# Weight halves split ahead, copies ahead of an exponential, squares kept in attention's order and masks moved, in a two-layer HGRN2 and attention step

## The chip, the cores and the metric

One core of a Trainium2 chip runs the whole kernel in one launch. The metric is the device time in microseconds (us); lower is better. The median of three runs of the kernel before is 1120.97 us (1120.49 to 1121.94).

## What is computed

Two layers are applied to a prompt of 512 rows and to 64 rows of eight sampled sequences, 1024 features each, all in fp32. Both layers have the same frame:

```python
h = rmsnorm(x, norm_w) * (1 + scale) + shift      # shift, scale, gate = silu(c) @ w_ada + b_ada
y = (mixer(h) * silu(z)) @ w_out                  # z: part of the layer's one input projection
x = x + gate * y
```

Layer 0 is a gated linear recurrence with 8 heads (key width 128, value width 256): `S_t = diag(f_t) S_{t-1} + k_t v_t^T`, `o_t = S_t^T q_t`, then an rmsnorm of `o` per head. Layer 1 is windowed attention with 12 heads of 128 in three groups with dilations 1, 4 and 16, with rotated, normalised queries and keys. The outputs are the new rows, the recurrent states, and the key and value rows of layer 1.

## The kernel before

The program is written by hand for five engines: TensorE (PE) multiplies, ScalarE (ACT) copies and evaluates functions, VectorE (DVE) and GpSimd (POOL) do the arithmetic between tiles, and SyncE (SP) issues nearly all transfers. Each engine runs its own list in program order, and semaphores tie the lists together. The order of each list is what the change edits.

**Weights.** They stream from HBM into `raw`, a ring of three slots. ScalarE copies a piece rounded to `w_hi` (`split_hi`, L347) and VectorE writes the rest to `w_lo` (`split_lo`, L355), both in rings of three slots. A product is three matmuls: high by high, high by low, low by high. `split_hi` waits until the piece three before it has been used; for a piece of an output column that is the end of the whole column (`pj_ready`), though the column has two pieces of eight blocks each. Once split, a slot of `raw` is free and SyncE can load the next piece.

**Layer 0, heads.** Step `h` of a loop projects head `h` and scans head `h - 1`. Within it, seven levels of decays are built: VectorE subtracts (`dve_sub`), ScalarE takes the exponential (`level_exps`, L895), VectorE multiplies keys and queries by it (`dve_level`, L867, L868). ScalarE's list also holds the copy of the values out of PSUM (L939) and of the turned keys (L943), both behind exponential 4 (counted from 0) in the steps that also scan. TensorE's chunk states (L1273) need both copies and, except for the last head, the masked keys of VectorE (`masked_keys`, L1098). In step 7, the last that projects, there are no adaLN projections on TensorE's list between the turned keys and the chunk states; steps 1 to 6 have them.

**Layer 0, output.** Eight columns `m` of 128 features, 16 blocks each (L1415). Column 0 is woven into the last scans; column 1's first eight blocks follow before the end of the loop. The second half of column 1 needs the piece `("out0", 1, 1)`. The residual input is parked in HBM and read back (`xT<-xpark`) when the last head is finished (`fin_done`). For each column VectorE adds the residual (`dve_residual`, L1182 to L1186), scales for the next norm (`amplify`, L575) and sums squares; ScalarE squares (`norm_square`, L535), writing in time order.

**Second norm.** TensorE sums squares over the partitions by a matmul with ones (`norm_pe`, L520), reading them through `perm`, which takes the time steps with a stride of 16 elements; its outputs are in the order of attention. ScalarE takes the inverse root (L550, L551), then VectorE scales (L583), ScalarE adds the shift and rounds (L557), VectorE forms the low part (L588), for eight feature blocks, then for the sequences' rows. Behind it VectorE has a weight split, `read_late_ada` (L488, L493), two masks (L2473, L2474) and a memset before its first step in attention.

**Attention.** TensorE starts with `pe_first_rows` as the blocks of `h` appear. `rope_act` sums squares per row, `rope_dve` (L1665, L1672) and `rope_pool` (L1692 to L1697) normalise and rotate; TensorE's next rows in the same PSUM bank (L1707) wait for L1665 and for the next split.

Of the kernel before, what the change touches and what calls it, by code (L numbers as in the profile page):

```python
# [128 lines left out]
def program(nc, I, O):  # L129
    with ExitStack() as ctx:  # L130
# [59 lines left out]
        at_done = sem("at_done")  # L190
# [143 lines left out]
        def split_hi(key):  # L334

            act = nc.scalar
            i = split_no[key][0]
            arrived(act, key)
            if i >= SPLITS:
                old = split_keys[i - SPLITS]  # L340
                if old[0] == "a" and old[2] in (0, 2, 4, 6):
                    act.wait_ge(half_used, 4 * old[1] + old[2] // 2 + 1)
                else:
                    act.wait_ge(pj_ready, split_no[old][1] + 1)
            n = index[key]
            size = stream[n][2] * stream[n][3]
            act.activation(w_hi[:, i % SPLITS, 0:size], raw[:, n % RAWS, 0:size], ACT.Copy).then_inc(hi_done, 1)  # L347
# [163 lines left out]
        def norm_pe(sq, slot):  # L511
            pe = nc.tensor
            if slot == 0:
                pe.wait_ge(sq_sum, 3 + KD - 2)
            else:
                pe.wait_ge(n_sq, 2 * KD)
            turned = perm(sq[:, slot, 0:TP])
            for e in range(2):
                out = X[:, e, 0:TP // 2].rearrange("p (r q i) -> p r q i", r=2, q=4)
                last = pe.matmul(out, ones[:], turned[:, 2 * e:2 * e + 2], start=(slot == 0), stop=(slot == 1))  # L520
                if slot:
                    last.then_inc(n_ms, 1)
            last = pe.matmul(X[:, 2, 0:TS], ones[:], sq[:, slot, TP:T], start=(slot == 0), stop=(slot == 1))
            last.then_inc(n_ms, 1)
# [5 lines left out]
        def norm_square(xT, sq, k):  # L530

            act = nc.scalar
            if k >= 2:
                act.wait_ge(sq_sum, 3 + k - 1)
            act.activation(sq[:, min(k, 1), :], xT[:, k, :], ACT.Square).then_inc(n_sq, 1)  # L535
# [9 lines left out]
        def second_norm_act(act, chain):  # L545
# [19 lines left out]
            split_hi(("a", 0, 2))  # L565
# [13 lines left out]
        def second_norm_dve(dve, chain):  # L579
# [11 lines left out]
            split_lo(("a", 0, 1))  # L591
# [21 lines left out]
            split_lo(("a", 0, 2))  # L613
            read_late_ada(chain)
# [262 lines left out]
        def act_step(act, chain, h):  # L877
# [30 lines left out]
            if end:  # L908
                if h <= AH:
                    logs_and_exps()  # L910
                act.wait_ge(ms_ready, f + 1)
                act.activation(sq0[:, 0, 0:TP], X[:, 0, :], ACT.Ln, bias=eps[:, 0:1], scale=1.0 / ADV)
                act.activation(sq0[:, 0, TP:T], X[:, 1, 0:TS], ACT.Ln, bias=eps[:, 0:1], scale=1.0 / ADV).then_inc(ms_read, 1)
                act.wait_ge(ms_read, f + 1)
                act.activation(sq0[:, 0, :], sq0[:, 0, :], ACT.Exp, scale=-0.5).then_inc(r_done, 1)
            if h == AH:
                oz_hi(6, 12)
                act.wait_ge(gram_ready, 3 * g + 3)
                act.wait_ge(op_ready, g)
                for i in (6, 7):  # L920
                    for s0_, s1_, t0_, t1_ in level_blocks(i):
                        ins = act.activation(at[s0_:s1_, :, t0_:t1_], wide_at(i)[s0_:s1_], ACT.Copy)
                ins.then_inc(at_done, 1)
            if h > AH:
                oz_hi(14, 16)
            if new:
# [10 lines left out]
                level_exps(0, 5 if scan else 6)  # L937
# [3 lines left out]
            if scan:  # L941
                act.wait_ge(kt_ready, g + 1)
                act.activation(kr[:].rearrange("p c k -> p (c k)"), X[:, 3, :], ACT.Copy).then_inc(kr_done, 1)  # L943
                if h == AH:
# [97 lines left out]
        def dve_step(dve, chain, h):  # L1042
# [59 lines left out]
            if new:  # L1102
# [3 lines left out]
                for i in range(8):  # L1106
# [4 lines left out]
                    if i == 5 and scan:  # L1111
                        masked_keys()
# [286 lines left out]
        def pe_out(pe, name, m, blocks):  # L1399
# [3 lines left out]
            for n in blocks:  # L1403
# [9 lines left out]
                for i, (a, b) in enumerate(((wh, o_hi(n)), (wh, lo), (wl, o_hi(n)))):  # L1413
                    for e, (x, z) in enumerate(((0, HP), (HP, T))):
                        last = pe.matmul(PJ[:, 2 * (t % 2) + e, 0:z - x], a[:, n % nk, :], b[:, x:z],  # L1415
                                         start=(n == 0 and i == 0), stop=(n == 2 * nk - 1 and i == 2))
            if blocks and blocks[-1] == 2 * nk - 1:
                last.then_inc(pj_ready, 1)
# [304 lines left out]
        def pe_first_rows(pe):  # L1723
# [40 lines left out]
            pe.wait_ge(ada_done, 4 + AH)  # L1764
# [195 lines left out]
        def pe_attention(pe, j):  # L1960
            a, old = j - 1, j > 0
            for k in range(12 if j < GH - 1 else 8):
                if k == 9:
                    pe.wait_ge(ss_mask, 3 * j + 1)
                if j == 0 and k < 2:
# [267 lines left out]
        def dve_attention(dve, chain, j):  # L2233
# [147 lines left out]
            for k in range(12 if j < GH - 1 else 8):  # L2381
                if k >= 8 or k % 2:
                    split_ahead(split_lo, j, k)
                if old and k == 0:
                    mask_s(a, 1)
                if k < 6:
# [70 lines left out]
        def attention_tables(dve, chain):  # L2457
# [11 lines left out]
            dve.tensor_copy(masks[1][0], masks[1][1])  # L2469

        def attention_masks(dve):

            dve.tensor_copy(masks[0][0], masks[0][1])  # L2473
            dve.tensor_copy(masks[2][0], masks[2][1]).then_inc(tab_done, 1)  # L2474
# [148 lines left out]
        def _(act):  # L2623
# [14 lines left out]
            for m in range(KD):  # L2638
                split_out(split_hi, "out0", m)
                if m == 0:  # L2640
                    split_hi(("out0", 1, 1))
                if m == KD - 1:
                    split_hi(("a", 0, 0))
                    split_hi(("a", 0, 1))
                wait_read(act, OUT0 + m)
                norm_square(xT1, nsq1, m)
# [13 lines left out]
        def _(dve):  # L2660
# [19 lines left out]
            dve.wait_ge(unparked, 16)  # L2680
            dve.tensor_copy(late_scT, scT[:])
            for m in range(KD):
                split_out(split_lo, "out0", m)
                if m == 0:
                    split_lo(("out0", 1, 1))
                if m == KD - 1:
                    split_lo(("a", 0, 0))
                if m == 4:
                    attention_tables(dve, chain)
                dve_residual(dve, chain, 0, OUT0 + m, m, xT1, yg)  # L2690
                amplify(m)
# [3 lines left out]
            attention_masks(dve)  # L2695
# [69 lines left out]
```

## Time and profile before

| | us |
|---|---|
| median of three runs | 1120.97 (1120.49 to 1121.94) |
| the profiled execution | 1122.75 |
| its span, first to last instruction | 1121.1 |
| outside the span | 1.65 |

The profile is one execution, told as a page (busy time of each engine, slices, the chain that ended last, groups of instructions) and as a trace that can be asked for waits, for a stretch in order of time, and for the granted clock of TensorE. Times in it count from the start of the span. A stall is the idle time in front of an instruction, with the event that ended it behind "<-". "issue" is idle time for which the profile shows no releaser. Instructions overlap a little, so the distance from start to start is less than a duration.

### The profile page before, as it was taken

What the parts mean: (1) busy time and instruction counts of PE and PEld (TensorE: products, weight loads), DVE (VectorE), ACT (ScalarE), POOL (GpSimd) and SP (SyncE); (2) the same over time, 40 slices, a digit from 0 to 9 for tenths busy, and PEclk for the clock granted to TensorE, in tenths of its full rate; (3) what the DMA queues carried; (4) which work ended last, traced back from release to release, by engine and by line L of the source; (5) the groups of instructions that cost most, each with busy time, mean ns of one, the idle gap of its engine ahead of it and who ended that gap; (6) DMA issues with size and microseconds to landing.
All of it is one profiled execution on the core that took longest, in us unless ns stands there. A gap on an engine that the chain in (4) does not pass through costs nothing.

```text
span 1121.1 us, 26202 instructions
## 1 busy us (share of the span) xinstructions
PE 1089.2 (97%) x11121; PEld 1038.6 (93%) x11121; DVE 635.8 (57%) x1280; ACT 505.1 (45%) x1035; POOL 151.0 (13%) x156
## 2 busy tenths in 40 slices
PE   8999999999999999998999999999999999999998
PEld 6799999999999998988998999999999999998997
DVE  3776676767585858673446634652455246437332
ACT  4653444445453545541124643653464365447122
POOL 1000010100000000000000730351045006300000
PEclk9999999999999999998999999999999999999999
DMA  9763444444544442219324455325623652263441
GB/s 321 282 206 110 142 134 149 137 144 128 153 126 147 134 136 77 81 52 273 104 76 142 117 134 152 100 71 118 166 77 97 152 138 80 60 156 87 152 113 47
DMA packets 232219, 147.73 MB, mean 132 GB/s; under 512 B 7876, under 2 KB 226206, under 8 KB 231591
## 3 DMA queue, kind: packets, MB, share of 16 engines
q1 hardware_dynamic: 217456, 134.17, 42.4%
q10 hardware_dynamic: 14646, 11.89, 3.2%
q8 instruction: 88, 1.44, 0.5%
q14 instruction: 29, 0.23, 0.1%
HBM read 124.00 MB, written 22.02 MB: 130 GB/s over the span
## 4 chain that ended last, share of the span: by engine, by line
PE 85%; DVE 6%; ACT 3%; issue 2%; DMA 2%; SPq 1%; ACTq 0%; DVEq 0%
PE PJ L382 26%; PE PJ L1707 18%; PE PJ L1415 15%; PE PJ L403 7%; PE X L1273 2%; PE X L1835 1%; PE X L1393 1%; PE X L1214 1%; PE X L1862 1%; PE PJ L685 1%; PE X L1395 1%; DMA pre<-in_ada_w_dram 1%; SPq L2521 1%; PE PJ L429 1%; PE X L1800 1%
## 5 line engine op out<-in xcount | busy, mean ns | idle before, releaser
L355 DVE TENSOR_TENSOR w_lo<-raw,w_hi 128x1024 fp32r<-128x1024 f32 (+1 forms) x128 | 157.0, 1239 | 163.0 <-ACT w_hi L347 162.1
L347 ACT ACTIVATE w_hi<-raw 128x1024 fp32r<-128x1024 f32 (+1 forms) x128 | 129.3, 1025 | 167.7 <-PE PJ L1707 69.9
L1707 PE MATMUL PJ<-w_hi,h_hi 128*128 128x256 f32 x600 | 167.3, 287 | 2.1 <-issue 1.4
L1707 PE MATMUL PJ<-w_lo,h_hi 128*128 128x256 f32 x600 | 164.6, 283 | 0.0
L382 PE MATMUL PJ<-h_hi,w_hi 128*128 128x288 f32 (+1 forms) x736 | 160.7, 300 | 0.6 <-ACT v_ L939 0.6
L382 PE MATMUL PJ<-h_hi,w_lo 128*128 128x288 f32 (+1 forms) x736 | 157.7, 296 | 0.0
L382 PE MATMUL PJ<-h_lo,w_hi 128*128 128x288 f32 (+1 forms) x736 | 157.4, 295 | 0.0
L1707 PE MATMUL PJ<-w_hi,h_lo 128*128 128x256 f32 x480 | 135.8, 283 | 0.0
L382 PEld LDWEIGHTS PJ<-h_hi,w_hi 128*128 128x128 f32 x736 | 118.1, 189 | 4.6 <-issue 3.1
L382 PEld LDWEIGHTS PJ<-h_hi,w_lo 128*128 128x128 f32 x736 | 118.9, 189 | 0.0
L382 PEld LDWEIGHTS PJ<-h_lo,w_hi 128*128 128x128 f32 x736 | 118.8, 189 | 0.0
L1707 PEld LDWEIGHTS PJ<-w_hi,h_hi 128*128 128x128 f32 x600 | 115.0, 192 | 2.8 <-issue 1.7
L1707 PEld LDWEIGHTS PJ<-w_lo,h_hi 128*128 128x128 f32 x600 | 115.0, 192 | 0.0
L1415 PE MATMUL PJ<-oz_low,w_hi 128*128 128x256 f32 x448 | 97.0, 299 | 0.0
L1707 PEld LDWEIGHTS PJ<-w_hi,h_lo 128*128 128x128 f32 x480 | 92.1, 192 | 0.0
L403 PE MATMUL PJ<-w_hi,h_hi 128*128 128x256 f32 x320 | 91.1, 292 | 0.8 <-DVE q_ L1060 0.8
L403 PE MATMUL PJ<-w_lo,h_hi 128*128 128x256 f32 x320 | 88.0, 283 | 0.0
L1415 PEld LDWEIGHTS PJ<-oz_low,w_hi 128*128 128x128 f32 x448 | 76.6, 192 | 0.0
L895 ACT ACTIVATE dd<-dd 128x576 f32<-128x576 f32 (+1 forms) x64 | 41.4, 658 | 69.0 <-DVE dd L1035 59.5
L403 PE MATMUL PJ<-w_hi,h_lo 128*128 128x256 f32 x256 | 72.4, 283 | 0.0
L1182 DVE SCALAR_TENSOR_TENSOR xT<-PJ,ada,xT 128x128 f32<-128x128 f32 (+1 forms) x40 | 17.8, 498 | 87.6 <-PE PJ L1415 87.6
L403 PEld LDWEIGHTS PJ<-w_hi,h_hi 128*128 128x128 f32 x320 | 61.2, 191 | 3.3 <-issue 1.6
(346 smaller groups left out, 2149.2 us busy)
## 6 DMA issues: line engine op xcount, KB each, us to landing
raw<-in_a_w_in_dram SPq DMA_DIRECT2D x48, 512.0 KB, 5.0
raw<-in_b_w_in_dram SPq DMA_DIRECT2D x64, 256.0 KB, 3.7
raw<-in_ada_w_dram SPq DMA_DIRECT2D x28, 512.0 KB, 3.9
kvc<-in_cache_kv_w_dram SPq DMA_DIRECT2D x24, 512.0 KB, 5.9
pre<-in_ada_w_dram SPq DMA_DIRECT2D x16, 512.0 KB, 10.1
s<-in_state_hgrn_dram SPq DMA_DIRECT2D x8, 1024.0 KB, 8.2
out_hgrn_sample_dram<-s ACTq DMA_DIRECT2D x8, 1024.0 KB, 5.0
raw<-in_a_w_out_dram SPq DMA_DIRECT2D x16, 512.0 KB, 5.0
```

The lines of the kernel that those rows point to most:

```text
L347: act.activation(w_hi[:, i % SPLITS, 0:size], raw[:, n % RAWS, 0:size], ACT.Copy).then_inc(hi_done, 1)
L355: dve.tensor_tensor(w_lo[:, i % SPLITS, 0:size], raw[:, n % RAWS, 0:size], w_hi[:, i % SPLITS, 0:size].bitcast(F32), ALU.subtract).then_in ...
L382: last = nc.tensor.matmul(PJ[:, 2 * s + e, 0:n1 - n0], a[:, k, :], b[:, k, n0:n1], start=(k == 0 and i == 0), stop=(k == KD - 1 and i == 2))
L403: last = nc.tensor.matmul(out_of(tile), a, b[:, k % 4, :], start=(k == 0 and i == 0), stop=(k == KD - 1 and i == len(passes) - 1))
L429: last = nc.tensor.matmul(PJ[q:q + 32, bank, n % 4 * P:n % 4 * P + P], scT[:, k, :], w[:, k, :], start=(k < 4), stop=(k >= 4))
L685: last = pe.matmul(PJ[:, 2 * t + e, 0:HT], a[:, k, :], b[:, k, e * HT:(e + 1) * HT], start=(k == 0 and i == 0), stop=(k == KD - 1 and i == 2))
L895: act.activation(dd[:, x % 2, 0:n], dd[:, x % 2, 0:n], ACT.Exp).then_inc(exp_done, 1)
L1182: dve.scalar_tensor_tensor(out=x, in0=y, scalar=gate, in1=x, op0=ALU.mult, op1=ALU.add)
L1214: last = pe.matmul(gram_at(i)[BL * q:BL * q + BL, n], left[:, t:t + BL], right[:, t:t + BL], start=True, stop=True)
L1273: last = pe.matmul(X[:, c // 2, c % 2 * ADV:(c % 2 + 1) * ADV], kr[:, c], v_[:, g % 2, c], start=True, stop=True)
L1415: last = pe.matmul(PJ[:, 2 * (t % 2) + e, 0:z - x], a[:, n % nk, :], b[:, x:z], start=(n == 0 and i == 0), stop=(n == 2 * nk - 1 and i == 2))
L1707: last = pe.matmul(PJ[:, tile // 2, tile % 2 * 256:tile % 2 * 256 + 256], a, b[:, k, :], start=(first and k == 0 and i == 0), stop=(kk == ...
```

## The change

- `split_hi` of a piece whose slot was last used by the first half of an output column of layer 0 now waits for that half (`half_out`, raised by TensorE after block 7) and no longer for the whole column. ScalarE splits `("out0", 1, 1)` straight behind the exponential of the last norm factor, ahead of the last two roundings of `oz`; VectorE splits it before it waits for the parked input.
- In the steps that project and scan, the value copy and the key copy stand ahead of exponential 4. In step 7 VectorE masks the keys one level earlier.
- `norm_square` writes in attention's order with two instructions instead of one, and the square of the last feature block moves to VectorE. `norm_pe` reads its operand contiguously.
- The first three attention pieces are split by ScalarE ahead of the second norm, the third by VectorE right behind the square of the last block. `read_late_ada` and two masks move into attention's first pass (its steps 3 and 6), with TensorE's wait for the first of them.

```diff
@@ split_hi
                 if old[0] == "a" and old[2] in (0, 2, 4, 6):
                     act.wait_ge(half_used, 4 * old[1] + old[2] // 2 + 1)
+                elif old[0] == "out0" and old[2] == 0:
+                    act.wait_ge(half_out, old[1] + 1)
                 else:
                     act.wait_ge(pj_ready, split_no[old][1] + 1)
@@ norm_pe
-            turned = perm(sq[:, slot, 0:TP])
             for e in range(2):
-                out = X[:, e, 0:TP // 2].rearrange("p (r q i) -> p r q i", r=2, q=4)
-                last = pe.matmul(out, ones[:], turned[:, 2 * e:2 * e + 2], start=(slot == 0), stop=(slot == 1))
+                last = pe.matmul(X[:, e, 0:TP // 2], ones[:], sq[:, slot, e * TP // 2:(e + 1) * TP // 2],
+                                 start=(slot == 0), stop=(slot == 1))
@@ norm_square
-            act.activation(sq[:, min(k, 1), :], xT[:, k, :], ACT.Square).then_inc(n_sq, 1)
+            slot = min(k, 1)
+            pairs = ((quarters(sq[:, slot, 0:TP]), perm(xT[:, k, 0:TP])), (sq[:, slot, TP:T], xT[:, k, TP:T]))
+            for out, x in pairs:
+                if eng is nc.scalar:
+                    ins = eng.activation(out, x, ACT.Square)
+                else:
+                    ins = eng.tensor_tensor(out, x, x, ALU.mult)
+            ins.then_inc(n_sq, 1)
@@ second_norm_act
-            split_hi(("a", 0, 2))
@@ second_norm_dve
-            split_lo(("a", 0, 1))
...
-            split_lo(("a", 0, 2))
-            read_late_ada(chain)
@@ act_step
+            if h > AH:
+                split_hi(("out0", 1, 1))
...
-                level_exps(0, 5 if scan else 6)
+                level_exps(0, 4 if scan else 6)
...
                 act.activation(kr[:].rearrange("p c k -> p (c k)"), X[:, 3, :], ACT.Copy).then_inc(kr_done, 1)
+                if new:
+                    level_exps(4, 5)
@@ dve_step
-                    if i == 5 and scan:
+                    if i == (5 if h < AH - 1 else 4) and scan:
                         masked_keys()
@@ pe_out
+                if layer == 0 and n == nk - 1:
+                    last.then_inc(half_out, 1)
@@ pe_first_rows
-            pe.wait_ge(ada_done, 4 + AH)
@@ pe_attention
+                if j == 0 and k == 7:
+                    pe.wait_ge(ada_done, 4 + AH)
@@ dve_attention
+                if j == 0 and k == 3:
+                    read_late_ada(chain)
+                if j == 0 and k == 6:
+                    attention_masks(dve, chain)
@@ ScalarE's list
                 split_out(split_hi, "out0", m)
-                if m == 0:
-                    split_hi(("out0", 1, 1))
-                if m == KD - 1:
-                    split_hi(("a", 0, 0))
-                    split_hi(("a", 0, 1))
-                wait_read(act, OUT0 + m)
-                norm_square(xT1, nsq1, m)
+                if m < KD - 1:
+                    wait_read(act, OUT0 + m)
+                    norm_square(act, xT1, nsq1, m)
+            for kk in range(3):
+                split_hi(("a", 0, kk))
@@ VectorE's list
-            dve.wait_ge(unparked, 16)
-            dve.tensor_copy(late_scT, scT[:])
             for m in range(KD):
                 split_out(split_lo, "out0", m)
                 if m == 0:
                     split_lo(("out0", 1, 1))
+                    dve.wait_ge(unparked, 16)
+                    dve.tensor_copy(late_scT, scT[:])
                 if m == KD - 1:
                     split_lo(("a", 0, 0))
+                    split_lo(("a", 0, 1))
...
                 dve_residual(dve, chain, 0, OUT0 + m, m, xT1, yg)
+                if m == KD - 1:
+                    wait_read(dve, OUT0 + m)
+                    norm_square(dve, xT1, nsq1, m)
+                    split_lo(("a", 0, 2))
                 amplify(m)
...
             second_norm_dve(dve, chain)
-            attention_masks(dve)
             dve.wait_ge(tab_done, 1)
```

## Rows read from the trace of the kernel before

**Rows 1.** First part of the page: busy time and share of each engine.

```profile
PE 1089.2 (97%) x11121; PEld 1038.6 (93%) x11121; DVE 635.8 (57%) x1280; ACT 505.1 (45%) x1035; POOL 151.0 (13%) x156
```

**Rows 2.** Waits of PE: line, releaser: total us, times, longest.

```profile
PE X L1273 <- ACT v_ L939: 2.9, 5, 0.6
```

**Rows 3.** Stretches: length, busy of PE, PEld, DVE, ACT, POOL, granted clock, DMA, GB/s.

```profile
448.00:450.00 2.00, 2.00 (x8) 1.62 (x6) 0.00 (x0) 0.00 (x0) 0.00 (x0) 0.50 0.00 0
...
516.00:518.00 2.00, 2.00 (x10) 2.00 (x10) 1.23 (x1) 0.32 (x1) 0.00 (x0) 0.50 0.89 202
...
620.00:625.00 5.00, 2.92 (x23) 2.54 (x22) 4.06 (x6) 3.74 (x13) 2.99 (x3) 1.00 0.74 209
```

**Rows 4.** Chain that ended last: start, us, engine, tile, line, count.

```profile
198.74 1.03 PE X L1304 x4
...
513.66 85.74 PE PJ L1415 x624
599.39 1.73 PE X L520 x4
...
602.30 1.05 PE X L520 x2
```

**Rows 5.** Order of time, step 2: start, us, instruction, count, idle before it.

```profile
168.72 0.63 ACT L895 ACTIVATE dd<-dd 128x512 f32<-128x512 f32 x1 [0.90 <-DVE dd L1035]
...
169.26 1.01 ACT L939 ACTIVATE v_<-PJ 128x1024 f32<-128x1024 f32 x1
...
170.16 0.59 ACT L943 ACTIVATE kr<-X 128x512 f32<-128x512 f32 x1
170.28 0.41 DVE L867 TENSOR_TENSOR qk<-k_,dd 128x256 f32<-128x256 f32 x1
...
170.85 1.97 PE L1273 MATMUL X<-v_,kr 128*128 128x256 f32 x8 [0.57 <-ACT v_ L939]
```

**Rows 6.** Order of time, step 7, where no adaLN projection stands between.

```profile
442.96 0.63 ACT L895 ACTIVATE dd<-dd 128x512 f32<-128x512 f32 x1 [3.51 <-DVE dd L1035]
...
445.93 0.59 ACT L943 ACTIVATE kr<-X 128x512 f32<-128x512 f32 x1
...
446.62 3.26 PE L1273 MATMUL X<-v_,kr 128*128 128x256 f32 x8 [2.12 <-ACT kr L943]
```

**Rows 7.** Order of time, output columns 1 and 2, and the residual of column 6.

```profile
512.18 0.29 DVE L2681 COPY vr<-scT 128x256 f32<-128x256 f32 x1 [7.31 <-DMA xT<-xpark]
512.39 1.22 DVE L355 TENSOR_TENSOR w_lo<-raw,w_hi 128x1024 fp32r<-128x1024 f32 x1
...
513.52 0.75 DVE L1182 SCALAR_TENSOR_TENSOR xT<-PJ,ada,xT 128x512 f32<-128x512 f32 x1
513.66 0.85 PE L1415 MATMUL PJ<-h_lo,w_hi 128*128 128x256 f32 x2 [5.19 <-DVE w_lo L355]
...
514.69 0.68 ACT L535 ACTIVATE nsq<-xT 128x576 f32<-128x576 f32 x1 [5.06 <-DVE xT L1186]
...
515.28 1.04 ACT L347 ACTIVATE w_hi<-raw 128x1024 fp32r<-128x1024 f32 x1
...
586.63 0.75 DVE L1182 SCALAR_TENSOR_TENSOR xT<-PJ,ada,xT 128x512 f32<-128x512 f32 x1 [7.60 <-PE PJ L1415]
```

**Rows 8.** Groups by line, shapes apart: busy, mean ns of one, idle before.

```profile
L575 DVE TENSOR_SCALAR kvc<-xT,amp 128x512 f32<-128x512 f32 x8 | 5.6, 699 | 0.3
...
L2061 ACT ACTIVATE qkT<-X 128x512 f32<-128x512 f32 x8 | 7.9, 1084 | 0.1
```

**Rows 9.** Order of time, end of the second norm and start of attention.

```profile
618.11 1.22 DVE L355 TENSOR_TENSOR w_lo<-raw,w_hi 128x1024 fp32r<-128x1024 f32 x1
...
619.82 1.04 ACT L347 ACTIVATE w_hi<-raw 128x1024 fp32r<-128x1024 f32 x1
...
621.07 0.69 DVE L1665 TENSOR_TENSOR rb<-PJ,oz 128x512 f32<-128x512 f32 x1
...
624.22 0.39 PE L1707 MATMUL PJ<-w_hi,h_hi 128*128 128x256 f32 x1 [0.70 <-DVE w_lo L355]
```

More of the change, by code:

```diff
@@ L189, in program @@
         sum_done, vs_done = sem("sum_done"), sem("vs_done")
-        at_done = sem("at_done")
+        at_done, half_out = sem("at_done"), sem("half_out")
         sub_done, exp_done, lv_done = sem("sub_done"), sem("exp_done"), sem("lv_done")
@@ L528, in logs_and_exps, with norm_square @@
             nc.scalar.preload_act_table_set("natural_log_exp_and_others")
-        def norm_square(xT, sq, k):
-            act = nc.scalar
+        def norm_square(eng, xT, sq, k):
             if k >= 2:
-                act.wait_ge(sq_sum, 3 + k - 1)
-            act.activation(sq[:, min(k, 1), :], xT[:, k, :], ACT.Square).then_inc(n_sq, 1)
+                eng.wait_ge(sq_sum, 3 + k - 1)
+            slot = min(k, 1)
[6 more added lines that the diff above has]
+            ins.then_inc(n_sq, 1)
         def add_square(sq, k):
@@ L2468, in attention_tables, with attention_masks @@
                                                     scalar=-1.0 if x == 0 else 1.0, in1=w2, op0=ALU.mult, op1=ALU.mult)
-            dve.tensor_copy(masks[1][0], masks[1][1])
-        def attention_masks(dve):
+            dve.tensor_copy(masks[1][0], masks[1][1]).then_inc(tab_done, 1)
+        def attention_masks(dve, chain):
             dve.tensor_copy(masks[0][0], masks[0][1])
-            dve.tensor_copy(masks[2][0], masks[2][1]).then_inc(tab_done, 1)
+            chain(dve.tensor_copy(masks[2][0], masks[2][1]))
         def load_attention_constants(sp):
```

## The prediction

> **What bounds the kernel now.** I read the first part of the page: TensorE is busy for 97% of the span and no other engine for 60% [rows 1], so an edit elsewhere pays only where it takes a stall out of TensorE's list, or where it makes TensorE's own instructions shorter. Then the waits of TensorE and, stretch by stretch, its stalls in order of time. Those that the diff touches are in four places: in front of the chunk states of steps 1 to 7 [rows 2, 5, 6], in the middle of output column 1 [rows 7], in the sums of squares [rows 4], and at the start of attention [rows 9]. Last the granted clock. It is at its upper level nearly everywhere; it stands at 0.50 (1.2 GHz instead of 2.4) behind just two stalls, that of step 7 (2.12 us) and that of column 1 (5.19 us) [rows 3, 6, 7]. Both are stalls that the change goes at, so a part of the gain is clock.
>
> **Steps 1 to 6.** ScalarE runs exponential 4, the value copy, the key copy; TensorE starts 0.1 us after the key copy, having stood still for 0.57 [rows 5]. The six steps stalled 0.49, 0.57, 0.57, 0.56, 0.58 and 0.57 us (five of them are the 2.9 us of [rows 2], the first has no releaser named). With the exponential behind both copies these start 0.54 us earlier at least (168.72 instead of 169.26), and earlier still, since ScalarE had been idle for 0.90 us before it and the projection's last matmul was out by 167.5. The keys are then copied by about 169.3, a microsecond before TensorE arrives at 170.28. All six stalls go: **-3.3**. The cost is the exponential: it now ends near 169.9 and its reader on VectorE starts at 170.28 anyway [rows 5], behind 0.4 us of other work. So nothing, with 0.4 us of cover. ScalarE's next level waits for TensorE and moves with it.
>
> **Step 7.** Here TensorE arrives at 444.5 and waits until 446.62. In the new order the value copy can start at 443.5, when exponential 3 is done [rows 6], the key copy at 444.4, done at 445.0: TensorE starts at 445.1. The masked keys, which the same matmuls await, would be next at 445.5; moved up a level they are done by 444.1, so it needs that edit too. Gain 1.5 us of stall. The eight matmuls took 3.26 us here and 1.97 in step 2 [rows 5, 6], at half the clock up to 450.5 [rows 3]; with the four behind them that is 1.6 us. The stall that is left (0.6) is like those of the steps before, behind which the clock held. **-3.1** (bounds -1.5, if the clock falls all the same, and -3.8, if no stall is left).
>
> **Output columns 1 and 2.** Column 1's second half waits for a split which VectorE makes at 512.39, because VectorE waits for the parked input first [rows 7]. In the new order ScalarE makes the high part at 499.7 (its slot's half column was used at 487.9) and VectorE the low part at 504.9 to 506.1, before TensorE wants it at 508.47. The stall of 5.19 goes. The clock too: from 513.66 to the end of column 7 it took 85.74 us [rows 4]; a column at full clock takes 599.39 - 586.63 = 12.8 [rows 4, 7], so six are 76.8 and the half column took 8.94 instead of 6.4, 2.5 too much.
>
> Not all of this 7.7 stays: **what is late next** is column 2's first piece. The parked input still lands at 512.1. VectorE then copies (0.21) and adds the residual, done 1.13 later at 513.5; ScalarE's square of column 0 starts at 513.57 (1.12 earlier than before) and the split stands behind it. With two squares for one, 0.70 instead of 0.59 from start to start, it starts at 514.27, and 2.26 us later both halves are done (1.04 high, 1.22 low): 516.53. TensorE is through with column 1 at 508.47 + 6.4 = 514.87. A new stall of 1.66 us: **-6.0**. The piece's transfer lands at 513.8, 0.5 us before ScalarE is free. Later pieces keep some 2 us of cover, since ScalarE splits them behind each column's square as now.
>
> Does the clock fall behind the new stall? The trace has no stall of that length amid dense matmuls. The nearest rows: 2.12 did it in step 7 and cost 1.6; 1.38 and 0.70 within 4 us, at 620 to 625, did not, the clock stays 1.00 with TensorE busy for 2.92 of 5.00 us [rows 3]. The second is nearer in kind (long matmuls on both sides) and in size (2.08 idle in all), so I take nothing; the other end is +2.5, what column 1 paid.
>
> **Second norm.** TensorE reads squares with a stride of 16: 512 columns took 1.73 us, where 576 contiguous ones of the same kind took 1.03 [rows 4], so 0.9 for 512. The first sum shortens by 0.8 and is followed by 1.0 us of late adaLN matmuls; it would reach the second sum at 601.3, but the last square, now on VectorE behind the residual (600.6 to 601.4), lets it in at 601.45 instead of 602.30. Its first half takes 0.43 less. So the inverse root starts 1.28 us earlier: **-1.3**. VectorE meanwhile has the square (0.8), the split of the third attention piece (1.15) and the scaling (0.8), free at 603.35, before the second root at 603.9. The rest of the stage keeps its pace; what follows shifts.
>
> **Squares, strided.** No row has ScalarE or two VectorE inputs read with a stride of 16 from SBUF. VectorE with one such input takes 699 ns for 512 elements, as contiguous ones do; ScalarE writing with such a stride takes 1084 where 590 is usual [rows 8]. I take the first for both, since it is a read; the other end is +0.5 us at each of the two squares on the path. The Trainium skill ("Advanced Engine Details and Errata", SBUF Cachelines) says that a line is 16 bytes and that reads need two hits on a line to be fast; stride 16 in fp32 has one hit. TensorE's doubled time per column agrees, VectorE's 699 does not; by the rule both squares would double, which is a rival below.
>
> **Start of attention.** VectorE's first step there (L1665) starts at 621.07, though ScalarE had its factors ready by 619.9 (its next instruction starts at 619.82) [rows 9]: before it stand the split at 618.11, the late adaLN read, two masks and a memset. With only the memset left VectorE is free 0.5 us behind the norm, at 617.4 with the 1.3 above, and the factors come at 618.6. So L1665 starts 2.4 us earlier, and the split behind it and TensorE's restart (624.22) with it: **-1.15** beyond the norm's. The work moved costs nothing at its new places: VectorE idles there by microseconds (0.55 us in step 3, 0.85 in step 6), and TensorE's wait for it moves four steps back. Freeing the raw slot of the third piece earlier lets SyncE load ahead; it then blocks for the cache load as before.
>
> **Sum.** 3.3 + 3.1 + 6.0 + 1.3 + 1.15 = 14.9 us. The profiled execution would go from 1122.75 to 1107.9; it lies 1.8 above the median of the runs, so against that I say 1120.97 - 14.9 = **1106.1**.
>
> **Rivals.**
> A, the forecast, 1106.1, its own range 1104.3 to 1107.5: **67%**.
> B, the clock falls behind the new stall of column 2. For it: 2.12 us sufficed in step 7. Against: 620 to 625. It costs 1.6 to 2.5: 1108.1. **14%**.
> C, strided reads at half pace: ScalarE's square 0.5 later lengthens the new stall to 2.2, VectorE's takes 0.6 of the norm's gain: 1107.2. **8%**.
> D, the reordering of copies does not do what it says, because TensorE meets another event just behind (gram reads, masked keys): 6.4 us do not come, 1112.5. Against it: masked keys are done at 169.7, before TensorE's 170.28. **8%**.
> E, slower. Exponential 4 now waits for two copies, and the second for TensorE's turned keys, which in turn wait for VectorE. From the point where the exponential ends behind 170.28 and VectorE has no slack left in the step, each of seven steps pays the copies and the exponential in series, 0.90 + 0.59 + 0.63 = 2.1, 14.8 in all, and D's gain is lost: 1120.97 - 8.5 + 14.8 = 1127.3. Against it: the 0.4 us of cover, and that VectorE waits for ScalarE again right after. **2%**.
> The last 1% is for gains and losses that cancel.
>
> The range, 1104.0 to 1109.6, holds A, B and C with their bounds and leaves out D and E. A measurement of this kernel can tell 0.2% (2.2 us) from no change: faster 0.97, same 0.01, slower 0.02.
>
> **What would show it.** Steps 1 to 6: no idle before L1273, step 7 about 0.6 and 1.97 us for the eight. Column 1: no stall, and a stall of 1.5 to 2.2 before column 2 with the split of its first piece as releaser; the granted clock behind it tells A from B. L520: half the time for 512 columns. L1665 about 1.2 us behind the norm's last step and TensorE's restart 0.8 behind the first rows. The prediction is wrong if the periods of steps 1 to 6 stay at 55.15 us, if the parked input lands late, or if a column's split shows as releaser in every column.

## The result, and the profile after

| | before | after |
|---|---|---|
| median of the runs, us | 1120.73 (1120.45 to 1121.94) | 1109.50 (1108.08 to 1112.19) |
| the profiled execution, us | 1122.75 | 1108.20 |
| its span, us | 1121.1 | 1106.6 |

The ratio is 0.9901, with a 95% interval of 0.9881 to 0.9921: 11.2 us less. The forecast was 14.9 less. Two later sets of runs of the same two kernels gave 11.9 and 11.6, so the shortfall of 3 to 4 us is real. The median after stands at the upper end of the forecast range (1104.0 to 1109.6) and outside the range of the forecast itself (1104.3 to 1107.5). The two profiled executions differ by 14.5 us, nearly the forecast. That agreement is partly chance: the profiled execution of before is slower than all the runs in the table, and that of after is near the fastest of its own. Where the 3 us went is what the experiments are about.

The page's first part and the waits of TensorE of the kernel after (line, releaser: total us, times, longest) answer [rows 1, 2]:

```profile
PE 1083.3 (98%) x11121; PEld 1034.7 (94%) x11121; DVE 638.6 (58%) x1282; ACT 508.2 (46%) x1041; POOL 151.3 (14%) x156
```

```profile
PE PJ L1422 <- DVE w_lo L357: 2.7, 1, 2.7
...
PE X L1280 <- ACT kr L948: 0.6, 1, 0.6
...
PE X L520 <- DVE nsq L541: 0.4, 1, 0.4
```

TensorE's own work is 5.9 us shorter (half clock and strided reads gone). The five waits of 2.9 us in front of the chunk states are gone; one of 0.6 is left, in step 7. On top now stands a wait that the kernel before did not have, in front of output column 2. In order of time (start, us, instruction, count, idle before it), steps 2 and 7 of after, the counterpart of [rows 5, 6]:

```profile
166.55 1.01 ACT L944 ACTIVATE v_<-PJ 128x1024 f32<-128x1024 f32 x1
...
167.46 0.59 ACT L948 ACTIVATE kr<-X 128x512 f32<-128x512 f32 x1
...
167.94 0.63 ACT L898 ACTIVATE dd<-dd 128x512 f32<-128x512 f32 x1
...
169.04 1.99 PE L1280 MATMUL X<-v_,kr 128*128 128x256 f32 x8
...
439.37 0.41 DVE L1105 TENSOR_TENSOR kz<-X,seqm 128x256 f32<-128x256 f32 x1
...
440.19 0.59 ACT L948 ACTIVATE kr<-X 128x512 f32<-128x512 f32 x1
...
440.87 1.97 PE L1280 MATMUL X<-v_,kr 128*128 128x256 f32 x8 [0.59 <-ACT kr L948]
```

The key copy is done at 168.05, a microsecond ahead of TensorE, and no idle time stands before L1280. In step 7 it is 0.59 instead of 2.12, and the eight matmuls take 1.97 us instead of 3.26. The parked input and output column 2, the counterpart of [rows 7]:

```profile
504.88 0.30 DVE L2697 COPY vr<-scT 128x256 f32<-128x256 f32 x1 [6.58 <-DMA xT<-xpark]
...
506.26 1.23 ACT L539 ACTIVATE nsq<-xT 128x512 f32<-128x512 f32 x2 [10.15 <-DVE xT L1193]
...
507.40 1.04 ACT L349 ACTIVATE w_hi<-raw 128x1024 fp32r<-128x1024 f32 x1
508.48 1.22 DVE L357 TENSOR_TENSOR w_lo<-raw,w_hi 128x1024 fp32r<-128x1024 f32 x1 [1.37 <-ACT w_hi L349]
...
509.75 0.53 PE L1422 MATMUL PJ<-h_hi,w_hi 128*128 128x256 f32 x2 [2.68 <-DVE w_lo L357]
```

Column 1 no longer waits. Column 2 waits for the split of its first piece, as forecast, but for 2.68 us and not 1.66: the squares hold ScalarE for 1.14 us (506.26 to 507.40) and not 0.70, and the parked input took longer. Behind the stall the granted clock (the value before the last two) stays at 1.00:

```profile
510.00:512.00 2.00, 2.00 (x17) 2.00 (x17) 1.54 (x5) 1.22 (x3) 0.00 (x0) 1.00 0.79 194
```

The second norm in order of time, and the strided squares in the groups by line (busy, mean ns of one, idle before), to be read beside [rows 4, 8]:

```profile
586.66 1.02 PE L520 MATMUL X<-nsq,ones 128*128 128x256 f32 x4
...
588.03 1.19 DVE L541 TENSOR_TENSOR nsq<-xT 128x512 f32<-128x512 f32 x2
...
589.15 1.21 DVE L357 TENSOR_TENSOR w_lo<-raw,w_hi 128x1024 fp32r<-128x1024 f32 x1
589.28 1.13 PE L520 MATMUL X<-nsq,ones 128*128 128x256 f32 x4 [0.42 <-DVE nsq L541]
```

```profile
L539 ACT ACTIVATE nsq<-xT 128x512 f32<-128x512 f32 x7 | 7.8, 1115 | 59.6 <-DVE xT L1193 59.6
...
L581 DVE TENSOR_SCALAR kvc<-xT,amp 128x512 f32<-128x512 f32 x8 | 5.5, 693 | 0.2
```

ScalarE needs 1115 ns for 512 strided elements where it took 0.68 us for 576 contiguous ones [rows 7]; VectorE's amplification, strided as well, still takes 693. At the end of the norm, the counterpart of [rows 9]:

```profile
604.08 0.69 DVE L616 TENSOR_TENSOR h_hi<-kvc,h_hi 128x512 fp32r<-128x512 f32 x1
...
606.53 0.69 DVE L1674 TENSOR_TENSOR rb<-PJ,oz 128x512 f32<-128x512 f32 x1 [1.11 <-ACT oz L1661]
...
609.68 0.39 PE L1716 MATMUL PJ<-w_hi,h_hi 128*128 128x256 f32 x1 [0.71 <-DVE w_lo L357]
```

L1674 now waits for its factors and for nothing of VectorE's own, and TensorE's restart comes with it.

### The profile page after: what moved, and what is told of

The parts are those of the page before. It is cut to its first block, busy times and chain, and to the rows that moved or that the text cites. A ratio compares the mean times of both kernels' runs of the same rounds, so it can differ in the third digit from the quotient of the medians.

```text
span 1106.6 us, 26211 instructions
## 1 busy us (share of the span) xinstructions
PE 1083.3 (98%) x11121; PEld 1034.7 (94%) x11121; DVE 638.6 (58%) x1282; ACT 508.2 (46%) x1041; POOL 151.3 (14%) x156
## 4 chain that ended last, share of the span: by engine, by line
PE 88%; DVE 4%; ACT 3%; DMA 2%; issue 1%; SPq 1%; ACTq 0%; DVEq 0%
PE PJ L384 27%; PE PJ L1716 18%; PE PJ L1422 14%; PE PJ L405 8%; PE X L1843 1%; PE X L1280 1%; PE X L1221 1%; PE X L1400 1%; PE X L1870 1%; PE PJ L688 1%; PE PJ L1744 1%; PE PJ L431 1%; PE X L1402 1%; DMA pre<-in_ada_w_dram 1%; PE X L1808 1%
```

## Experiments

Each kernel was timed beside the kernel before, in three sets (medians 1120.74, 1121.44 and 1120.76 us). In the brackets behind a median stand the lowest and highest run, where given, the ratio to the kernel before and its 95% interval. Stretches are lines of: length, busy of PE, PEld, DVE, ACT, POOL, granted clock, DMA, GB/s.

### The kernel after, repeated

`again` and `after3` are the changed kernel without an edit, beside the kernels of the first and the third set.

> The changed kernel once more, unaltered, for the spread of its executions (1108.1 to 1112.2 us so far, where the kernel before spreads over 1.5 us). Theory 1, the clock: behind the new stall in front of output column 2 (2.68 us in the profiled execution, clock at its upper level throughout) TensorE's clock falls in some executions and not in others; a fall costs 2 to 4 us. Then the executions form two groups some 2 to 4 us apart, the mean granted clock is lower in the slower group (0.995 to 0.997 against 0.998 to 0.999), and the median lies between 1108 and 1111. Rival, the transfers: the parked input lands at a different time in each execution and the stall is as long as it is late; then the times are spread evenly and the mean clock is the same in all.

> The changed kernel once more beside the two others of this call, as their measure: 1108.8 to 1109.5.

Measured: 1108.83 (1108.63 to 1109.02; 0.9890, 0.9875 to 0.9904) and 1109.14 (1107.54 to 1110.24; 0.9892, 0.9876 to 0.9909). The stall before column 2 was 2.93 and 2.03 us. The parked input took 9.69 and 8.76 us from its issue to VectorE's use of it (9.46 in the profile above), and the stall moves with it: 0.93 more transfer, 0.90 more stall. The two groups of executions, 2 to 4 us apart, that the first expectation describes did not appear in `again` (0.4 us from lowest to highest); in `after3` two executions at a mean clock of 1.000 (1107.54 and 1108.68) lie below two at 0.998 (1109.61 and 1110.24). The clock held behind this stall in all three profiles of the changed kernel. The twelve executions of the three sets together have a median of 1108.8 us, the 41 of the kernel before 1120.8: 12.0 less.

### The copies ahead of the exponential, alone

```diff
-                level_exps(0, 5 if scan else 6)
+                level_exps(0, 4 if scan else 6)
...
+                if new:
+                    level_exps(4, 5)
...
-                    if i == 5 and scan:
+                    if i == (5 if h < AH - 1 else 4) and scan:
```

> The kernel before with the edit of the heads alone: exponential 4 behind the copies of values and keys in steps 1 to 7, masked keys one level earlier in step 7. By the prediction 3.3 us in steps 1 to 6 and 3.1 in step 7, of which 1.6 is clock: 1120.7 - 6.4 = 1114.3 us. Without the clock's part (it falls in step 7 all the same, or it did not fall in every execution of the kernel before) 1115.9. Rival: the gain of the heads is given back at the next wait; then above 1118.

Measured: 1116.07 (0.9953, 0.9938 to 0.9968), 4.7 less. In its profile steps 1 to 7 look as in the kernel after. The 4.7 is what the stalls alone should give (3.3 + 1.5), without step 7's 1.6 us of clock. The interval, 3.6 to 6.9 us, holds the forecast 6.4 too, so this run alone doesn't decide it. The kernels `tail` and `tailhalf` below leave steps 1 to 7 as before, and their traces show why. First `tail`: TensorE's first instruction behind the same stall, and the stretches behind it; then the same stretches of `tailhalf`:

```profile
446.04 1.32 PE L1274 MATMUL X<-v_,kr 128*128 128x256 f32 x5 [2.12 <-ACT kr L944]
```

```profile
446.00:448.00 2.00, 1.96 (x10) 1.78 (x11) 0.99 (x3) 0.22 (x1) 0.00 (x0) 1.00 0.00 0
448.00:450.00 2.00, 2.00 (x20) 2.00 (x19) 0.74 (x2) 1.32 (x3) 0.00 (x0) 1.00 0.00 0
```

```profile
446.00:448.00 2.00, 2.00 (x6) 1.54 (x6) 0.68 (x2) 0.00 (x0) 0.00 (x0) 0.50 0.00 0
448.00:450.00 2.00, 2.00 (x12) 1.72 (x11) 0.00 (x0) 0.22 (x2) 0.00 (x0) 0.70 0.00 0
```

The stall is 2.12 us in both, as in the kernel before. In one execution the clock stays at 2.4 GHz, in the other it falls to 1.2. Of the four profiled executions with this stall (before, `col1`, `tail`, `tailhalf`) it fell in two. From the chunk states of step 7 to those of step 8 these two take 35.7 and 35.9 us and the other twelve profiles 33.6 to 34.2, so the fall costs about 1.8. The kernel before has two kinds of executions among its 37 in the three sets: 24 have a mean granted clock of 0.996 or 0.997 and a median of 1120.6 us, 13 have 0.993 to 0.995 and a median of 1122.2. The profiled execution (1122.75, mean clock 0.995) is like the 13; the median is not. That step 7's clock makes this distance of 1.6 us fits its price, but is not shown. The mean does not tell where the clock fell: a fall at the end of attention (below) lowers it as much and costs 1.2, the fall in column 1 costs anything from 1.5 to 2.3 (below), and TensorE's clock also stands at 0.50 near the end of the span, behind its last matmul, where it costs nothing, for 0.4 to 3.7 us by profile.

### Output column 1's second piece split ahead, alone

```diff
+                elif old[0] == "out0" and old[2] == 0:
+                    act.wait_ge(half_out, old[1] + 1)
...
+            if h > AH:
+                split_hi(("out0", 1, 1))
...
-            dve.wait_ge(unparked, 16)
-            dve.tensor_copy(late_scT, scT[:])
             for m in range(KD):
...
                     split_lo(("out0", 1, 1))
+                    dve.wait_ge(unparked, 16)
+                    dve.tensor_copy(late_scT, scT[:])
```

> The kernel before with one part of the change: output column 1's second piece is split ahead (ScalarE behind the last exponential, VectorE before it waits for the parked input). If the terms of the sum hold by themselves: minus 5.2 us of stall, minus 2.5 of half clock behind it, plus a new stall in front of column 2 (squares are contiguous here, so 1.7 to 2.5): about 1115.0, and 1117 if the clock falls behind the new stall as well. If the clock's share is not to be had (as the run with the copies alone gave 4.7 of 6.4), about 1117.

Measured: 1116.34 (1114.88 to 1118.27; 0.9960, 0.9946 to 0.9973), 5.1 less, with an interval of 3.0 to 6.1 that holds the forecast of 6.0; the median lies between the two values of the expectation and does not choose. The stall of 5.2 and its half clock are gone, and in front of column 2 stand 1.94 us, behind which the clock fell in this execution:

```profile
514.56 0.53 PE L1419 MATMUL PJ<-h_hi,w_hi 128*128 128x256 f32 x2 [1.94 <-DVE w_lo L357]
```

```profile
516.00:518.00 2.00, 2.00 (x11) 2.00 (x10) 1.84 (x4) 1.22 (x2) 0.00 (x0) 0.51 0.62 172
```

### Both of these, without the norm and attention part

> The changed kernel without its norm and attention part: only the copies and masked keys, and column 1's second piece split ahead. The two parts alone gave -4.7 and -5.1; if they add up, 1121.0 - 9.8 = 1111.2, and the changed kernel beside it is 2.0 to 2.4 faster. If the two share a gain (a fall of the clock that each takes away), more: 1110.

Measured: 1110.62 (0.9905, 0.9891 to 0.9919), 10.1 less; 4.7 and 5.1 add up to 9.8. So the changed kernel's norm and attention part brings 1.5 us in the same set (1110.62 to 1109.14), a difference that the two intervals do not separate. From the first sum of squares to L1674 the traces give 21.83 us in `notail`, 19.87 in after and 19.86 in `after3`, 2.0 less. The strided squares take 0.5 of it back in front of column 2 (below).

### The norm and attention part alone

This is the kernel before with the squares' order, the last square on VectorE, the three attention pieces split ahead and the late reads and masks moved.

> The kernel before with the other part: squares in attention's order, the last one on VectorE, three attention pieces split ahead, late adaLN read and masks moved. The prediction's sum gives -2.45 (1118.3); by the traces of the changed kernel the two terms were 0.8 and 1.2, so -2.0 (1118.7). Nothing before output column 1 should change.

Measured: 1122.29 (1120.36 to 1123.85; 1.0008, 0.9999 to 1.0016). No gain at all: from the first sum of squares to attention's first step on VectorE the trace has 22.12 us instead of 21.84. The end of column 7 in its trace:

```profile
595.57 1.03 PE L518 MATMUL X<-nsq,ones 128*128 128x256 f32 x4
595.83 2.00 ACT L347 ACTIVATE w_hi<-raw 128x1024 fp32r<-128x1024 f32 x2 [8.53 <-PE PJ L1416]
...
596.92 1.23 DVE L355 TENSOR_TENSOR w_lo<-raw,w_hi 128x1024 fp32r<-128x1024 f32 x1 [8.18 <-ACT w_hi L347]
...
598.06 0.75 DVE L1183 SCALAR_TENSOR_TENSOR xT<-PJ,ada,xT 128x512 f32<-128x512 f32 x1
...
600.43 1.13 PE L518 MATMUL X<-nsq,ones 128*128 128x256 f32 x4 [2.66 <-DVE nsq L539]
```

ScalarE can split the second attention piece only when column 7 has ended, since its slot was last used by the first piece of that column. VectorE's half of that split (596.92) stands in front of the last residual (598.06), and TensorE waits 2.66 us for the last square. The chain is visible; the next kernel tests it by adding one wait of the other part:

```diff
+                elif old[0] == "out0" and old[2] == 0:
+                    act.wait_ge(half_out, old[1] + 1)
                 else:
                     act.wait_ge(pj_ready, split_no[old][1] + 1)
```

> The kernel of the run with the norm and attention part alone, with one line of column 1's part added: the wait of split_hi on the half column instead of the whole (no piece is split at another place in the lists). In the run without it ScalarE's splits for attention waited for the end of column 7, VectorE's residual behind them ran about 4.9 us later than before and TensorE stood 2.66 us in front of the second sum. If that wait is what ate the part's gain, the 2.66 falls to about 0.4 and the time from 1122.3 to 1119 (the two norm and attention terms as measured in the changed kernel, -2.0 against the kernel before). If the part gives nothing for another reason, it stays at 1122.

Measured: 1119.40 (1116.38 to 1121.50; 0.9987, 0.9976 to 0.9998), 1.4 less than before; the interval, 0.2 to 2.7, holds the 2.0 that the trace gives (19.87 us instead of 21.84). The wait is 0.42 again and the residual starts 0.20 us behind the end of the column instead of 2.49 (so it had been 2.3 late in `tail`, and not the 4.9 of the expectation):

```profile
598.22 1.02 PE L520 MATMUL X<-nsq,ones 128*128 128x256 f32 x4
598.42 0.75 DVE L1185 SCALAR_TENSOR_TENSOR xT<-PJ,ada,xT 128x512 f32<-128x512 f32 x1 [4.03 <-PE PJ L1418]
...
600.85 0.48 PE L520 MATMUL X<-nsq,ones 128*128 128x256 f32 x1 [0.42 <-DVE nsq L541]
```

So the norm's part needs the half column's wait. The prediction costed `half_out` at column 1 only and did not see this tie; in the changed kernel, where both are there, it cost the sum nothing.

### The squares back in time order

```diff
-            pairs = ((quarters(sq[:, slot, 0:TP]), perm(xT[:, k, 0:TP])), (sq[:, slot, TP:T], xT[:, k, TP:T]))
+            pairs = ((sq[:, slot, :], xT[:, k, :]),)
```

with `norm_pe` reading through `perm` again.

> The changed kernel with the squares written in time order again, one contiguous instruction on either engine, and TensorE reading them with a stride of 16 as before. If reading with a stride costs ScalarE 0.5 us and VectorE 0.45 (1.23 us for the pair on ScalarE, 1.19 on VectorE in the changed kernel's profile), ScalarE's split of column 2's first piece starts 0.55 us earlier and the stall shrinks from 2.7 to 2.1 us, while the two sums on TensorE take 0.8 and 0.4 us longer and the last square 0.45 less: the profiled time is the same within 0.7 us, and the stall of 2.1 us lets the clock fall less often, so that the median is lower than that of the changed kernel by up to 1.5 us. If the stride costs nothing and two instructions instead of one are the price, the pair still falls from 1.23 to 0.69.

Measured: 1109.70 (0.9895, 0.9881 to 0.9910), beside 1108.83 of `again`. ScalarE's square is 0.69 us again and VectorE's 0.76; the stall before column 2 is 2.48 with a parked transfer of 9.78, where `again` has 2.93 with 9.69, so 0.5 of the stall is the strided square. TensorE's first four matmuls on the squares take 1.89 us again instead of 1.02, and from the end of column 7 to the first scaling it is 5.17 us instead of 4.47. By the traces attention's order gains 0.7 in the norm and gives 0.5 back at column 2; the medians do not tell the two kernels apart, and the lower median that the expectation had did not come. In the profile the clock fell behind the stall:

```profile
510.00:512.00 2.00, 2.00 (x10) 2.00 (x10) 1.93 (x6) 1.31 (x2) 0.00 (x0) 0.50 0.66 157
```

### The stall in front of column 2: one order turned, and lengthened

`mid`: ScalarE splits column 2's first piece ahead of column 0's square.

> The changed kernel with one order turned: ScalarE splits column 2's first piece ahead of column 0's square, not behind it; no load is moved. If the strided square on ScalarE in front of the split (1.14 us) is what lengthens the new stall, it falls from 2.7-2.9 to about 1.6 and the time by 1.1, to 1107.7. If the parked input alone sets it, the stall and the time stay (1108.8).

Measured: 1109.25 (1107.22 to 1110.69; 0.9890, 0.9877 to 0.9904): no gain that can be told. ScalarE now waits for the piece's own transfer, which lands at 507.69, behind the parked input (505.43):

```profile
507.69 1.06 ACT L349 ACTIVATE w_hi<-raw 128x1024 fp32r<-128x1024 f32 x1 [10.68 <-DMA raw<-in_a_w_out_dram]
```

The stall is 2.10. Neither theory of this expectation holds as written: behind the square stands the piece's own transfer, almost as late.

`stall4`: two more squares of column 0 on ScalarE ahead of that split, their results overwritten.

```diff
                     wait_read(act, OUT0 + m)
+                    if m == 0:
+                        chain(act.activation(nsq1[:, 0, :], xT1[:, 0, :], ACT.Square))
+                        chain(act.activation(nsq1[:, 0, :], xT1[:, 0, :], ACT.Square))
```

> The changed kernel with two more squares of column 0 on ScalarE ahead of the split of column 2's first piece (about 0.8 us each, results unused): the stall in front of column 2 grows from 2.7-2.9 to about 4.4. If the clock falls behind that stall only by its length, it falls in every execution now: 1108.8 + 1.6 + 1.6 to 2.5 of half clock, 1112 to 1113, with a granted clock of 0.50 behind the stall in the profile. If the clock does not depend on this stall, 1110.4.

Measured: 1110.94 (1109.72 to 1112.17; 0.9907, 0.9893 to 0.9920), 1.7 above `mid`. The stall is 3.21 with a parked transfer of 8.59, so 1.4 longer than it would be with that transfer; the clock fell behind it. The 1112 to 1113 of a fall in every execution was not reached, and this run doesn't settle how often it falls.

### No stall in front of column 2

SyncE issues the parked input one piece later, behind the load of column 2's first piece, and both engines split that piece before they turn to the parked input:

```diff
-                if key == ("out0", 1, 1):
+                if key == ("out0", 2, 0):
...
-                split_out(split_hi, "out0", m)
+                if m != 1:
+                    split_out(split_hi, "out0", m)
+                if m == 0:
+                    split_hi(("out0", 2, 0))
...
+                    split_lo(("out0", 2, 0))
                     dve.wait_ge(unparked, 16)
```

> The changed kernel with the first piece of output column 2 loaded, and split on both engines, before the parked input is waited for: the transfer of the parked input is issued behind that piece's, and the two splits stand ahead of ScalarE's square of column 0 and of VectorE's wait. Theory 1 (one new stall, 2.7 us, and the clock behind it in some executions): no stall in front of column 2, clock at its upper level in every execution, 1105.4 us in the profiled one and the spread below 1 us; against the changed kernel's median of 1109.5 that is 4 us. Rival (the parked input is what bounds this stretch): the stall moves to the next wait of TensorE, column 3 or the PSUM banks of column 2, and the median stays above 1107.5.

> The version without a stall in front of column 2 once more: 1106.3, about 2.5 below the changed kernel. If its lead was a matter of chance in the clock, under 1 us of it is left.

Measured: 1106.33 (1105.59 to 1106.82; 0.9866, 0.9849 to 0.9882), and in the third set 1106.58 (1104.81 to 1107.39; 0.9868, 0.9853 to 0.9882): 2.5 and 2.6 us less than the changed kernel beside it. Column 2's piece is split at 501.3 to 503.6, the parked input lands at 504.83 as before, and TensorE has no stall there. This version beats the kernel before by 14.3 us and the changed kernel by 2.5 us; its eight executions (1104.81 to 1107.39) all lie below the eight of the changed kernel beside them (1107.54 to 1110.24).

```profile
502.39 1.23 DVE L357 TENSOR_TENSOR w_lo<-raw,w_hi 128x1024 fp32r<-128x1024 f32 x1 [3.53 <-ACT w_hi L349]
504.83 0.29 DVE L2702 COPY vr<-scT 128x256 f32<-128x256 f32 x1 [1.21 <-DMA xT<-xpark]
505.04 0.74 DVE L1189 SCALAR_TENSOR_TENSOR xT<-PJ,ada,xT 128x512 f32<-128x512 f32 x1
```

Its executions still lie 2.6 us apart, so the spread below 1 us and the clock that never falls, which the expectation had, did not come. Their mean granted clock is 1.000 or 0.999 from 1104.81 to 1106.00 us, and 0.997 or 0.998 from 1106.65 to 1107.39. Both profiles show the place of a fall, the end of attention, behind two stalls of 0.61 and 0.95 us that every kernel here has:

```profile
1006.99 0.27 PE L1917 MATMUL X<-ident,oz 64*128 64x64 f32 x1 [0.61 <-DVE oz L2373]
...
1008.58 0.63 PE L1907 MATMUL X<-ident,p 128*128 128x128 f32 x4 [0.95 <-ACT pt L2086]
```

```profile
1008.00:1010.00 2.00, 1.42 (x11) 1.45 (x12) 1.40 (x2) 2.00 (x5) 0.00 (x0) 0.90 0.00 0
1010.00:1012.00 2.00, 2.00 (x12) 2.00 (x11) 1.66 (x3) 2.00 (x5) 0.00 (x0) 0.50 0.02 4
```

In the kernel after the same two (0.60 and 0.95) left the clock at 1.00. Of the fourteen profiles of this study it fell here in six. From L1674 (L1665) to the end of the span these six take 500.9 to 501.5 us and the other eight 499.7 to 500.3: a fall here costs 1.2.

## Why the prediction was right and wrong

The direction and all the places were right. The size was not: 14.9 us forecast, 11.2 to 11.9 measured. The step that failed, as far as the runs show it, is the clock: the sum takes the half clock that the one profiled execution shows at full size and subtracts it from the median of the runs, though that execution lay 1.95 us above the median of its kernel (1122.75 against 1120.8). Some 0.9 us more are mis-sized terms, the new stall and the norm above all. By the prediction's own steps:

**Steps 1 to 6: 3.3 forecast.** Right. The chunk states of step 6 start at 390.6 to 391.5 in the four profiles with the old order and at 387.2 to 388.0 in the ten with the new (means 390.9 and 387.4): 3.5. The exponential cost nothing, as said. Rivals D and E fell with it.

**Step 7: 3.1 forecast, 1.5 + 1.6.** The stall was right to 0.1 (2.12 to 0.59). The clock term is what failed: I read it from the profiled execution and subtracted it from the median. It is there in that execution: from the first matmul on `v_,atz` to the next projection TensorE takes 7.38 us before and 4.25 after, 3.1 less. It is not there in every execution: of four profiles with this stall the clock fell in two, and the run with the copies alone gave 4.7 of 6.4 (interval 3.6 to 6.9). How often it fell in the unprofiled executions stays open. The prediction wrote down that the profiled execution lay 1.8 us above the median, and did not ask what the 1.8 was. That was the warning: terms that may exist only in the profiled execution can't be taken from the median.

**Output columns 1 and 2: 6.0 forecast, 5.1 alone and 5.4 on top of the copies (10.1 less 4.7).** The 5.2 us stall and its clock are gone. The clock fell behind a stall of about 5 us in all four profiles that have one, but the 2.5 for it is again the size of one execution. From the first matmul behind the stall to the end of column 7 they take 85.6, 85.1, 84.8 and 85.3 us; at full clock it would be 76.9 for six columns and 6.4 for the half. So the fall costs 2.3 in the kernel before (the prediction subtracted an end from a start and got 2.5), 1.8 in `heads`, 1.5 in `tail` and 2.0 in `tailhalf`, and stall and clock together 6.4 to 7.5, on average 7.0. The stall that takes its place was mis-sized: 2.03 to 2.93 and not 1.66. Of the excess 0.4 to 0.5 is the strided square (1.14 from start to start and not 0.70), which was part of rival C, and the rest, up to 0.8, the parked transfer: 8.8 to 9.7 us here, 8.9 in the profile of before. The prediction took its length as fixed, though it ends the stall.

**The clock behind the new stall: 0 forecast.** Of the eight profiles with this stall it fell in four (1.94, 2.10, 2.48 and 3.21 us: `col1`, `mid`, `sqtime`, `stall4`) and held in four (2.03, 2.50, 2.68 and 2.93: `after3`, `notail`, after, `again`). The changed kernel itself is in the second four with all its three profiles, so for it rival B, at 14%, is possible in other executions and not shown. The length doesn't decide it within this range. From the first matmul of column 2 to the end of column 7 it is 76.9 us in the four where it held and 78.4 in all four where it fell, so a fall costs 1.5 here. Taking one row (620 to 625 in [rows 3]) as evidence that it holds was the wrong kind of argument; it was a question of how often. The Trainium skill ("TensorE: Matmul & The Clock Gate", Part 1) says of the start of a kernel that the number of its slow matmuls differs from run to run, with the phase of the gate. The profiles show such a difference in the middle of a kernel too: 2.12 us in step 7, two fell, two held.

**Second norm: 1.3 forecast, 0.8 measured** (from the end of column 7 to the inverse root, 4.15 us before and 3.35 after). TensorE's part is as said. VectorE's pair of squares takes 1.12 from start to start and not 0.8, so the second sum waits 0.42. This is rival C again, which had 8%: of all rivals it is the one that the traces bear out, 0.4 to 0.5 us at column 2 and 0.4 in the norm. What misled is the choice of row: [rows 8] has one strided input on VectorE at full pace, and the prediction carried it over to ScalarE and to an instruction with two strided inputs. Neither holds: ScalarE takes 1.12 us for 512 strided elements where 576 in a row took 0.69, and VectorE 1.06 where its products of 512 in a row take 0.69. The Trainium skill ("Advanced Engine Details and Errata", SBUF Cachelines) says that reads want two hits on a line to be fast, and gives no size for engine or instruction; ScalarE's 1115 ns and VectorE's square agree, VectorE's one-input amplification, 693 ns, does not.

**Start of attention: 1.15 forecast.** Right: from the inverse root to VectorE's first step 17.69 us before and 16.52 after, 1.17.

**The sum again**, with the sizes measured and against the median: 3.5 + 1.5 for the copies, without step 7's clock; 7.0, the average of four profiles, less the new stall of 2.0 to 2.9 for the columns; 2.0 for norm and attention. That is 11.1 to 12.0 with the clock held behind the new stall, where the medians have 11.2 to 11.9 and all executions together 12.0. No fall behind the new stall is needed for it. If it fell in half of the executions, at 1.5 each, 10.3 to 11.2 would be left, which fits the first set alone; this is not excluded.

The prediction's own marks read: no idle before L1280 in steps 1 to 6, yes; 0.6 and 1.97 in step 7, yes; a stall of 1.5 to 2.2 before column 2, its releaser yes, its size no; L520 at half the time, 1.02 for four instead of 1.89, yes; TensorE's restart 0.7 behind, yes. The granted clock was to tell A from B: in the three profiles of the changed kernel it told A, in four of the five of its relatives with such a stall B.

## What to carry to other kernels

Before a term of clock, or any term that a single profiled execution shows, is subtracted from a median, ask how that execution stands to the others: here it lay 1.95 us above their median, as much as one fall of the clock costs. When a wait is taken away, cost the wait behind it with its own spread: a transfer that ends a stall has no fixed length, and the best kernel here came from moving the transfer's issue and the split ahead of it together, where moving the split alone gave nothing. An edit can be free only because another one is there: undo each part in turn before calling it harmless.

## What the runs showed that was not expected

- TensorE's clock can fall to 1.2 GHz, or not, behind the same stall in kernels that hardly differ there: 2.12 us twice and twice; 1.9 to 3.2 us in four of eight; two short ones of 0.6 and 0.95 us, 1.6 apart, in six of fourteen. Behind about 5 us it fell in all four. A fall costs this kernel 1.2 to 2.3 us; the executions of the changed kernel spread over 4.7, from 1107.5 to 1112.2, and how much of that is clock is not shown.
- 512 elements in fp32 with a stride of 16: ScalarE's activation 1115 ns, VectorE's product of a strided input with itself 1058 ns, VectorE's product with a scalar 693 ns, TensorE 1.89 us for 512 columns instead of 1.02.
- The parked transfer of 2.3 MB took 8.6 to 9.8 us from its issue to VectorE's use of it in the fourteen profiles.
